# Hybrid encoder layer: expert rows added to the output by accumulating scatters, expert weights in 4 KB pieces, nested branches, hidden products transposed in the gate bank

## The chip, the cores and the metric

The kernel runs on one core of a Trainium2 chip, as one launch. The metric is the device time of that launch in microseconds (us). Engines are called as in the profile: PE (TensorE; PEld its weight loads), DVE (VectorE), ACT (ScalarE), POOL (GpSimd) and SP (SyncE, which here only issues DMAs). All data are float32.

## What is computed

One encoder layer over 512 tokens of width 1024: attention of two kinds, an output projection, and then a hierarchical mixture of experts. Each token picks one of 4 groups of experts, and two of the 4 experts in that group.

```python
def hier_moe(h, w_rg, b_rg, w_re, b_re, w_gate, w_up, w_down):
    ...
    pg_top, g_idx = lax.top_k(p_g, 1)                  # one group of 4
    ...
    pe_top, e_idx = lax.top_k(p_e, TOP_K_IN_GROUP)     # two experts in it
    wts = pg_top * pe_top / jnp.sum(pe_top, axis=-1, keepdims=True)
    ...
    a = jnp.einsum('bsd,edf->bsef', h, w_gate)
    u = jnp.einsum('bsd,edf->bsef', h, w_up)
    hid = jax.nn.silu(a) * u * combine[..., None].astype(h.dtype)
    return jnp.einsum('bsef,efd->bsd', hid, w_down)

x = x + mixed @ w_out[l]
h2 = rms_norm(x, g_ffn_norm[l])
x = x + hier_moe(h2, ...)      # 16 experts, D_EXPERT = 256, 512 tokens x 2 experts
```

## The kernel before

**Stages.** Up to about 340 us the kernel computes the projections, the two attentions and the output projection. Tokens stand in four blocks of 128 (T = 4); `x_sb[:, t, :]` holds the residual stream. Near the end of the attention, block by block, the router is computed: `logits_out(t)` picks group and experts, `ranks_out(t)` gives each token its slot in each of its two experts, and `dispatch(t)` (POOL, two indirect DMAs) scatters the normed rows `h2s[t]` to the DRAM tensor `slot_rows`.

**Items.** Every expert has CAP = 96 slots. The 16 x 96 slots are cut into ITEMS = 12 items of 128 slots; three items hold the 4 experts of one group. What doesn't fit goes to extra tiles of one expert each: 10 are provided for, the first (item 12, LAST) is always computed, the others stand under branches (`passes`). An item is four blocks of 32 slots, each with the weights of its own expert.

**An item on the engines.** PE: `x_turns` (8 transposes of the gathered rows, L1401), `gate_up` (64 matmuls, L1416), `hid_turns` (2 transposes of the hidden products, L1424), `down` (32 matmuls, L1437). ACT: silu (L732) and the left half of y out of the bank (`left_y`, L738). DVE: `x_read` (L1074), `hidden` (L1083), `hidden_read` (L1090), `right_y` (L1097). ACT issues the load of the item's rows (L722) and the store of y to the DRAM tensor `expert_rows` (L743). y_sb has two buffers. PE runs the items in this order:

```python
x_turns(0)
for g in range(LAST + 1):
    gate_up(g)
    if g < LAST:
        x_turns(g + 1)
    if g > 0:
        down(g - 1)
    hid_turns(g)
down(LAST)
```

**Weights.** SP loads an expert's gate and up weights (`load_gu`, L367, 2048 KB) and down weights (`load_dn`, L371, 1024 KB) into a ring of RING = 5 experts. A load is issued when the last item that uses the buffer's former expert has run its matmuls. A partition's 16 KB (8 KB for down) are one piece.

**The end.** When the last y is stored, POOL goes through the branches of the extra tiles (L313, L315) and gathers for each token block its two rows of `expert_rows` (8 indirect DMAs, L575); DVE multiplies each by its weight and adds it to `x_sb` (8 instructions, L1125); SP stores the four blocks to `out` (L438). The weights come from `weights_out(t)` (L954 to L957: four small DVE instructions), which before run inside item 1. Early on, two DMAs zero `slot_rows` and most of `expert_rows`. The order is written by hand; engines wait on semaphores.

## Time and profile before

| | us |
|---|---|
| median of 3 runs (571.57 to 580.37) | 573.88 |
| profiled execution | 577.23 |
| its span, first to last instruction | 575.5 |
| PE busy in the span | 498.2 |
| end of the last matmul | 541.87 |

The profiled execution has 1.73 us around its span. Stage times below are microseconds from the span's start.

### The profile page before, as it was taken

What the parts mean: (1) busy time and instruction counts of PE and PEld (TensorE: products, weight loads), DVE (VectorE), ACT (ScalarE), POOL (GpSimd) and SP (SyncE); (2) the same over time, 40 slices, a digit from 0 to 9 for tenths busy, and PEclk for the clock granted to TensorE, in tenths of its full rate; (3) what the DMA queues carried; (4) which work ended last, traced back from release to release, by engine and by line L of the source; (5) the groups of instructions that cost most, each with busy time, mean ns of one, the idle gap of its engine ahead of it and who ended that gap; (6) DMA issues with size and microseconds to landing.
All of it is one profiled execution on the core that took longest, in us unless ns stands there. A gap on an engine that the chain in (4) does not pass through costs nothing.

```text
span 575.5 us, 7543 instructions
## 1 busy us (share of the span) xinstructions
PE 498.2 (87%) x2858; PEld 262.2 (46%) x2858; DVE 232.8 (40%) x591; ACT 112.0 (19%) x273; POOL 134.7 (23%) x150
## 2 busy tenths in 40 slices
PE   5898899999989999999999969369999999999600
PEld 3553544445656676655666655323333333333100
DVE  1127345505697534544455653333421122211133
ACT  2200332233213343313223220300000001000100
POOL 2211388732899100000010211303100000000050
PEclk9999899999998999999999967559999999999955
DMA  8999910006000000470002493636999999970165
GB/s 303 422 386 420 422 56 0 1 1 235 1 1 1 0 1 2 183 329 1 0 1 71 160 354 105 241 110 202 338 419 423 424 425 423 427 303 38 76 235 209
DMA packets 21501, 111.53 MB, mean 194 GB/s; under 512 B 3152, under 2 KB 4688, under 8 KB 16720
## 3 DMA queue, kind: packets, MB, share of 16 engines
q1 hardware_dynamic: 13680, 88.68, 38.5%
q10 hardware_dynamic: 4320, 13.83, 6.1%
q0 software_dynamic: 3456, 8.39, 4.1%
q8 instruction: 31, 0.51, 0.4%
q14 instruction: 14, 0.11, 0.1%
HBM read 81.53 MB, written 33.55 MB: 200 GB/s over the span
## 4 chain that ended last, share of the span: by engine, by line
PE 74%; DVE 7%; issue 4%; DMA 3%; ACT 1%; POOL 1%; POOLq 1%; DVEq 0%; ACTq 0%
PE bank L1416 17%; PE bank L1164 12%; PE bank L1302 10%; PE bank L1437 8%; PE bank L1139 7%; PE bank L1226 5%; PE bank L1240 4%; PE bank L1267 3%; PE bank L1199 3%; PE bank L1401 2%; DMA arena<-expert_rows,small 2%; PE bank L1254 1%; POOL arena L575 1%; PE bank L1424 1%; PE bank L1316 1%
## 5 line engine op out<-in xcount | busy, mean ns | idle before, releaser
L1164 PE MATMUL bank<-arena 128*128 128x512 f32 (+1 forms) x256 | 115.2, 589 | 5.5 <-DVE arena L783 3.1
L1416 PE MATMUL bank<-arena 128*32 128x512 f32 x832 | 96.3, 608 | 1.4 <-DVE arena L1074 0.8
L1139 PE MATMUL bank<-arena 128*128 128x128 f32 (+1 forms) x412 | 61.0, 284 | 20.8 <-DVE arena L865 4.6
L1164 PEld LDWEIGHTS bank<-arena 128*128 128x128 f32 x256 | 49.6, 196 | 61.4 <-issue 54.6
L1139 PEld LDWEIGHTS bank<-arena 128*128 128x128 f32 (+1 forms) x412 | 50.2, 144 | 56.9 <-issue 42.8
L1302 PE MATMUL bank<-arena 128*128 128x512 f32 x128 | 63.5, 624 | 0.0
L1416 PEld LDWEIGHTS bank<-arena 128*32 128x32 f32 x832 | 27.0, 112 | 61.4 <-issue 59.9
L865 DVE COPY arena<-bank 128x512 f32<-128x512 f32 (+2 forms) x64 | 36.2, 586 | 35.7 <-PE bank L1139 35.7
L1437 PE MATMUL bank<-arena 128*32 128x512 f32 x416 | 47.4, 595 | 0.8 <-DVE arena L1090 0.8
L575 POOL DMA_INDIRECT arena<-expert_rows,small x8 | 8.4, 1053 | 144.8 <-issue 144.8
L457 POOL TENSOR_SCALAR small<-small 128x1 f32<-128x1 f32 x16 | 3.7, 232 | 157.5 <-ACT arena L638 95.8
L1083 DVE TENSOR_TENSOR arena<-arena,bank 128x256 f32<-128x256 f32 x13 | 5.5, 421 | 82.2 <-ACT arena L732 76.8
L1226 PE MATMUL bank<-arena 96*128 96x512 f32 x64 | 35.2, 634 | 1.0 <-ACT arena L624 1.0
L473 POOL TENSOR_TENSOR arena<-arena 128x512 f32<-128x512 f32 (+2 forms) x20 | 22.1, 1119 | 59.1 <-issue 18.9
L674 ACT ACTIVATE arena<-bank,small 128x512 f32<-128x512 f32 x32 | 22.0, 687 | 70.4 <-DVE small L969 70.3
L969 DVE TENSOR_REDUCE small<-bank 128x1 f32<-128x512 f32 x32 | 22.0, 686 | 33.7 <-PE bank L1226 33.7
L1302 PEld LDWEIGHTS bank<-arena 128*128 128x128 f32 x128 | 22.9, 197 | 22.1 <-issue 22.1
L1240 PE MATMUL bank<-arena 128*128 128x64 f32 x256 | 32.3, 270 | 0.0
L453 POOL TENSOR_TENSOR small<-small 128x24 f32<-128x24 f32 (+2 forms) x7 | 29.8, 4261 | 6.5 <-DVE small L823 3.5
L1240 PEld LDWEIGHTS bank<-arena 128*128 128x128 f32 x256 | 31.2, 192 | 0.2 <-issue 0.2
L783 DVE TENSOR_TENSOR arena<-bank,small 128x512 f32<-128x512 f32 (+1 forms) x28 | 18.1, 666 | 28.8 <-PE bank L1139 28.7
L732 ACT ACTIVATE arena<-bank 128x256 f32<-128x256 f32 x13 | 5.0, 383 | 124.1 <-PE bank L1416 124.1
(148 smaller groups left out, 506.3 us busy)
## 6 DMA issues: line engine op xcount, KB each, us to landing
arena<-in_w_gu SPq DMA_DIRECT2D x17, 2048.0 KB, 13.8
arena<-in_w_dn SPq DMA_DIRECT2D x17, 1024.0 KB, 13.8
slot_rows<-arena SPq DMA_DIRECT2D x1, 11264.0 KB, 36.3
arena<-slot_rows ACTq DMA_DIRECT2D x13, 512.0 KB, 9.5
expert_rows<-arena ACTq DMA_DIRECT2D x13, 512.0 KB, 10.1
expert_rows<-arena SPq DMA_DIRECT2D x1, 4608.0 KB, 45.5
arena<-in_w_out SPq DMA_DIRECT2D x2, 2048.0 KB, 8.2
arena<-in_x SPq DMA_DIRECT2D x4, 512.0 KB, 10.8
```

The source lines that it names most:

```text
L453: nc.gpsimd.tensor_tensor(v, v, mhalf[:, 0:n], ALU.pow).then_inc(s_root, 1)
L473: nc.gpsimd.tensor_tensor(dst, src, src, ALU.mult).then_inc(s_sqr, 1)
L674: nc.scalar.activation(Pb[u % 2], SB[u % 2][:, :], ACT.Exp, bias=nmax[:, u % 2, h:h + 1], accum_out=ssum[:, t % 2, 0, h:h + 1]).then_inc(s ...
L865: nc.vector.tensor_copy(PT[u % 2][:, 0:blocks, :], TPB[p % 2][:, 0:blocks * P].rearrange("p (a b) -> p a b", a=blocks))\
L969: nc.vector.tensor_reduce(nmax[:, u % 2, u % H:u % H + 1], SB[u % 2][:, :], AX.X, ALU.max, negate=True).then_inc(s_mx, 1)
L1139: last = nc.tensor.transpose(TPB[p % 2][0:s.shape[-1], b * P:(b + 1) * P], s, ident)
L1164: last = nc.tensor.matmul(product_bank(i)[:, 0:width], hT[:, k, t * P:(t + 1) * P], w[:, k, :], start=(k == 0), stop=(k == KD - 1))
L1226: nc.tensor.matmul(SB[u % 2][:, :], qT[:, h, t * P:(t + 1) * P], kT[:, h, :], start=True, stop=True).then_inc(s_S, 1)
L1240: last = nc.tensor.matmul(OB[t % 2][:, h * DV:(h + 1) * DV], PT[u % 2][:, k, :], v_sb[:, k, h * DV:(h + 1) * DV], start=(k == 0), stop=(k ...
L1302: last = nc.tensor.matmul(YB[b][:, :], src[:, k, :], w_o[half][:, k, b * 512:(b + 1) * 512], start=(k == 0), stop=(k == 3))
L1416: last = nc.tensor.matmul(GU[g % 2][BLK * b:BLK * (b + 1), :], xT[g % 2][:, k, BLK * b:BLK * (b + 1)], w_gu[n % RING][:, k, :], start=(k = ...
L1437: last = nc.tensor.matmul(YR[g % 2][half][BLK * b:BLK * (b + 1), :], hidT[g % 2][:, k, BLK * b:BLK * (b + 1)], w_dn[n % RING][:, k, half * ...
```

## The change

**Output by accumulating scatters.** SP stores `x_sb` to `out` right after the output projection. Each item's y is multiplied by its row's weight when it leaves PSUM (`left_y`, `right_y`, now with `tag_sb[:, g, 1:2]` as scale) and POOL then adds the rows to `out` by indirect DMAs with `compute_op=ALU.add` (`add`). Row number and weight reach the slot's partition as "tags": POOL scatters pairs (row, weight) to a DRAM tensor `slot_tags` just as it scatters the rows, and ACT reads them back (`load_tags`). An item mixes two experts, in which the same token can stand twice, so each item has two adds ("runs"), one for each expert; the rows of the other have their number pushed out of bounds by a constant (`K_CUT`) and are skipped. Adds of different experts in a group are kept apart by waits (`added`). y_sb has three buffers, released by the adds. `expert_rows`, the gathers L575, the DVE adds L1125 and the stores after them are gone, and so is the zeroing of `expert_rows`. `weights_out(t)` moves from item 1 to behind `ranks_out(t)`, with its exponentials (`top_exps`) on ACT.

**Weights in pieces of 4 KB.** The host lays them out so that each partition's 16 KB (8 KB) are four (two) pieces.

**Nested branches.** The branches of the extra tiles are nested; the first that isn't taken skips all.

**Gate bank.** `hid_turns` writes into the gate half of the item's own bank `GU[g % 2]`. `x_turns(1)` writes to `YR[1]` and comes ahead of `gate_up(0)`; from then on `x_turns` run two items ahead, behind `down`, and ACT loads an item's rows four ahead.

```diff
-        y_sb = [at(110, D_MODEL), at(114, D_MODEL)]
-        y_back = [[at(kb + 4 * i, D_MODEL) for i in (0, 1)] for kb in (16, 24, 48, 56)]
+        y_sb = [at(110, D_MODEL), at(114, D_MODEL), at(136, D_MODEL)]
...
+        def added_before(g):
+
+            return 16 * sum(2 if i < ITEMS else 1 for i in range(g % 3, g, 3))
...
-            for i in range(1, EXTRA):
-                with eng.If(tiles > i):
+            with ExitStack() as more:
+                for i in range(1, EXTRA):
+                    more.enter_context(eng.If(tiles > i))
                     extra(ITEMS + i)
...
-            sp.dma_start(y_dram[(ITEMS + 1) * P:, :].rearrange("(r p) d -> p r d", p=P),
-                         zero.unsqueeze(1).to_broadcast([P, EXTRA - 1, D_MODEL])).then_inc(s_zero, 16)
+            sp.wait_ge(s_fill, 1)
+            sp.dma_start(tag_dram.rearrange("(p r) c -> p (r c)", p=P), tag_fill).then_inc(s_zero, 16)
...
-                sp.dma_start(w_gu[n % RING].rearrange("p k f -> p (k f)"),
+                sp.dma_start(w_gu[n % RING].rearrange("p (q k) f -> p q (k f)", q=4),
...
             sp.wait_ge(s_y, len(groups))
             load_gu(4, 4)
+            for t in range(T):
+                sp.wait_ge(s_x1, group["b", t, 1] + 1)
+                sp.dma_start(out[t], x_sb[:, t, :]).then_inc(s_out, 16)
...
-            for t in range(T):
-                sp.wait_ge(s_fin, t + 1)
-                sp.dma_start(out[t], x_sb[:, t, :]).then_inc(s_out, 16)
             sp.wait_ge(s_out, 16 * T)
+            sp.wait_ge(s_add[LAST % 3], added_before(LAST) + 16)
...
+            def dispatch_tags(t, of, done, rows):
+                for k in range(TOP):
+                    nc.gpsimd.indirect_dma_start(
+                        out=tag_dram, out_offset=bass.IndirectOffsetOnAxis(ap=of[:, t, k:k + 1], axis=0),
+                        in_=tags[:, t, k, :], in_offset=None,
+                        bounds_check=rows * P - 1, oob_is_err=False).then_inc(done, 16)
+
+            def early_tags(t):
+                pool.wait_ge(s_wts, t + 1)
+                dispatch_tags(t, slots[0], s_tagged, ITEMS)
...
             dispatch(3)
+            for t in range(T):
+                early_tags(t)
...
+                dispatch_tags(t, slots[1], s_over, TILES)
+
+            pool.wait_ge(s_out, 16 * T)
+
+            def add(g, run):
+                pool.wait_ge(s_ya, g + 1)
+                pool.wait_ge(s_yv, g + 1)
+                pool.wait_ge(s_tok, 1 if g < ITEMS else 2)
+                nc.gpsimd.indirect_dma_start(
+                    out=out_rows, out_offset=bass.IndirectOffsetOnAxis(ap=tag_row[:, run, g:g + 1], axis=0),
+                    in_=y_sb[g % 3], in_offset=None,
+                    bounds_check=SEQ - 1, oob_is_err=False, compute_op=ALU.add).then_inc(s_add[g % 3], 16)
+
+            def added(g, run):
+
+                pool.wait_ge(s_add[g % 3], added_before(g) + 16 * (run + 1))
+
+            for g in range(0, ITEMS, 3):
+                add(g, 0)
+                added(g, 0)
+                add(g, 1)
+                add(g + 1, 0)
+                added(g, 1)
+                added(g + 1, 0)
+                add(g + 1, 1)
+                add(g + 2, 0)
+                added(g + 1, 1)
+                added(g + 2, 0)
+                add(g + 2, 1)
+            added(LAST - 1, 1)
+            add(LAST, 0)
...
-            for t in range(T):
-                for k in range(TOP):
-                    nc.gpsimd.indirect_dma_start(
-                        out=y_back[t][k], out_offset=None, in_=y_dram,
-                        in_offset=bass.IndirectOffsetOnAxis(ap=slots[2][:, t, k:k + 1], axis=0),
-                        bounds_check=(ITEMS + EXTRA) * P - 1, oob_is_err=False).then_inc(s_back[t], 16)
...
+            act.wait_ge(s_tagged, 16 * TOP * T)
+            load_tags(0, ITEMS)
...
+                act.wait_ge(s_tag, 16 if g < ITEMS else 32)
+                if g >= 3:
+                    act.wait_ge(s_add[g % 3], added_before(g))
+                nc.scalar.activation(y_sb[g % 3][:, 0:512], YR[g % 2][0][:, :], ACT.Copy,
+                                     scale=tag_sb[:, g, 1:2]).then_inc(s_ya, 1)
...
                 hidden(g)
-                if g < LAST:
-                    x_read(g + 1)
                 if g > 0:
                     right_y(g - 1)
+                if g + 2 <= LAST:
+                    x_read(g + 2)
                 hidden_read(g)
                 if g == 0:
                     slots_out()
-                if g == 1:
-                    for t in range(T):
-                        weights_out(t)
+                    tag_rows(0, ITEMS)
+                if g == LAST - 1:
+                    tag_rows(ITEMS, TILES)
...
             x_turns(0)
+            x_turns(1)
             for g in range(LAST + 1):
                 gate_up(g)
-                if g < LAST:
-                    x_turns(g + 1)
                 if g > 0:
                     down(g - 1)
+                if g + 2 <= LAST:
+                    x_turns(g + 2)
                 hid_turns(g)
             down(LAST)
```

**What moves on POOL.** Ahead, POOL's rows of before from the dispatch of the last two blocks to the end of its straight code (L538 is `dispatch`, L561 the second scatter of the rows that didn't fit, L313 and L315 the first branch).

```order
L538 DMA slot_rows<-arena,small 2816x1024 x4
L561 DMA slot_rows<-arena,small 2816x1024 x8
L313 TENSOR_LOAD small
L313 ISA x2
L315 COMPARE_AND_BRANCH
```

And the same place of the change (L551 is `dispatch`, L558 `dispatch_tags`, L587 the second scatter of rows, L599 `add`).

```order
L551 DMA slot_rows<-arena,small 2816x1024 x4
L558 DMA slot_tags<-small 2816x2 x8
L587 DMA slot_rows<-arena,small 2816x1024 x2
L558 DMA slot_tags<-small 2816x2 x2
...
L599 DMA out<-arena 512x1024 x25
L324 TENSOR_LOAD small
L324 ISA x2
L327 COMPARE_AND_BRANCH
```

POOL gets 8 tag scatters behind the dispatch, 8 more among the second scatters (the pair of rows stands four times in all), and 25 adds ahead of the branches.

**What moves on PE.** PE's rows of before from the start of the expert stage (the two last matmul groups of the router end above it).

```order
L1401 MATMUL bank<-arena 128x128 x8
L1416 MATMUL bank<-arena 32x512 x32
L1401 MATMUL bank<-arena 128x128 x8
L1424 MATMUL bank<-arena 128x128 x2
L1416 MATMUL bank<-arena 32x512 x32
L1401 MATMUL bank<-arena 128x128 x8
L1437 MATMUL bank<-arena 32x512 x16
L1424 MATMUL bank<-arena 128x128 x2
```

And of the change (L1463 is `x_turns`, L1478 `gate_up`, L1485 `hid_turns`, L1498 `down`).

```order
L1463 MATMUL bank<-arena 128x128 x16
L1478 MATMUL bank<-arena 32x512 x32
L1463 MATMUL bank<-arena 128x128 x8
L1485 MATMUL bank<-arena 128x128 x2
L1478 MATMUL bank<-arena 32x512 x32
L1498 MATMUL bank<-arena 32x512 x16
L1463 MATMUL bank<-arena 128x128 x8
L1485 MATMUL bank<-arena 128x128 x2
```

Item 1's transposes now stand ahead of the first gate matmuls, and each later item's one place earlier; the last items have none left to do (where the trace counts 64 gate matmuls and 32 down matmuls for an item, the order counts 32 and 16).

**What moves on DVE.** DVE's rows of before from the slots of block 1 to the attention output of block 3 (L948 ends `ranks_out(1)`, L874 and L877 are `attn_out(1, 3)`, L783 the reads of the transposes).

```order
L948 CAST small<-small 128x2
L874 RECIPROCAL small<-small 128x8
L877 TENSOR_TENSOR arena<-bank,small 128x512
L783 TENSOR_TENSOR arena<-bank,small 128x512
```

And of the change (L1006 ends `ranks_out(1)`, L1012 to L1015 are `weights_out(1)`, L932 and L935 `attn_out(1, 3)`).

```order
L1006 CAST small<-small 128x2
L1012 TENSOR_SCALAR arena<-arena 128x1
L1013 TENSOR_TENSOR arena<-arena 128x1
L1014 RECIPROCAL small<-arena 128x1
L1015 TENSOR_TENSOR small<-small,arena 128x1
L932 RECIPROCAL small<-small 128x8
L935 TENSOR_TENSOR arena<-bank,small 128x512
L841 TENSOR_TENSOR arena<-bank,small 128x512
```

Four small instructions come between the ranks of block 1 and the attention output of block 3.

## Rows read from the trace of the kernel before

**Rows 1.** The page's busy times and shares of the span.

```profile
PE 498.2 (87%) x2858; PEld 262.2 (46%) x2858; DVE 232.8 (40%) x591; ACT 112.0 (19%) x273; POOL 134.7 (23%) x150
```

**Rows 2.** Stages: start:end, length, busy by engine, granted clock, DMA share, GB/s.

```profile
360.00:380.00 20.00, 7.44 (x40) 6.92 (x40) 5.66 (x39) 4.61 (x15) 4.05 (x5) 0.56 0.64 246
420.00:440.00 20.00, 20.00 (x182) 6.81 (x178) 4.26 (x8) 1.35 (x3) 0.00 (x0) 1.00 1.01 420
480.00:500.00 20.00, 20.00 (x186) 6.81 (x182) 4.26 (x8) 1.35 (x3) 0.00 (x0) 1.00 1.02 427
540.00:576.00 36.00, 1.83 (x20) 0.32 (x12) 10.96 (x9) 0.58 (x1) 8.43 (x8) 0.59 0.53 193
```

**Rows 3.** Chain that ended last, expert stage: start us, us, what.

```profile
371.12 3.31 DMA slot_rows<-arena,small
...
377.98 1.95 PE bank L1401 x8
...
380.70 9.92 PE bank L1416 x64
...
418.91 7.00 PE bank L1416 x64
425.91 1.02 PE bank L1401 x8
426.94 3.57 PE bank L1437 x32
430.50 0.37 PE bank L1424 x2
...
502.67 7.00 PE bank L1416 x64
...
538.19 3.69 PE bank L1437 x32
541.90 0.70 DVE arena L1097
...
542.67 3.15 DMA expert_rows<-arena
...
558.37 9.45 DMA arena<-expert_rows,small
```

**Rows 4.** DMA issues at 328, 371, 548 and 474 us: op xcount, KB each, us to landing.

```profile
slot_rows<-arena,small POOLq DMA_INDIRECT x1, 10.7
...
slot_rows<-arena,small POOLq DMA_INDIRECT x1, 3.3
...
arena<-expert_rows,small POOLq DMA_INDIRECT x1, 4.4
...
arena<-in_w_gu SPq DMA_DIRECT2D x1, 2048.0 KB, 15.8
```

**Rows 5.** DMA issues by line, from the page.

```profile
arena<-in_w_dn SPq DMA_DIRECT2D x17, 1024.0 KB, 13.8
arena<-slot_rows ACTq DMA_DIRECT2D x13, 512.0 KB, 9.5
expert_rows<-arena ACTq DMA_DIRECT2D x13, 512.0 KB, 10.1
```

**Rows 6.** Tile expert_rows from 400 us on, stores and gathers together: times to landing.

```profile
DMA to landing us min/median/max: 2.6/7.6/11.9
```

**Rows 7.** Timeline of POOL from 396 us: start, us, instruction, idle before.

```profile
396.35 0.96 POOL L561 DMA_INDIRECT slot_rows<-arena,small  x1 [24.27 <-DVE small L1066]
...
405.23 0.96 POOL L561 DMA_INDIRECT slot_rows<-arena,small  x1 [0.30 <-issue]
```

**Rows 8.** Timeline of DVE at the moved instructions and at the end.

```profile
342.42 0.17 DVE L948 CAST small<-small 128x2 int32<-128x2 f32 x1
342.49 0.20 DVE L874 RECIPROCAL small<-small 128x8 f32<-128x8 f32 x1
...
408.82 0.14 DVE L954 TENSOR_SCALAR arena<-arena 128x1 f32<-128x1 f32 x1
...
537.11 0.69 DVE L1097 COPY arena<-bank 128x512 f32<-128x512 f32 x1 [2.60 <-PE bank L1437]
```

More of the change, by code:

```diff
@@ L166, in build @@
         logits = sm(T, E)
-        wts = sm(T, TOP)
-        slots = [sm(T, TOP).bitcast(i32) for _ in range(3)]
+        tags = sm(T, TOP, 2)
+        tag_fill = sm(2 * TILES)
+        slots = [sm(T, TOP).bitcast(i32) for _ in range(2)]
         slot_f = sm(3, T, TOP)
@@ L986, in _ @@
             dve.wait_ge(s_k, 16)
+            for k in range(TOP):
+                link(nc.vector.tensor_copy(tags[:, :, k, 0], konst[:, K_ROW:K_ROW + T]))
             dve.wait_ge(s_bm, 1)
@@ L1018, in _ @@
                     ranks_out(RANKS_AT[s])
+                    weights_out(RANKS_AT[s])
             attn_out(1, T - 1)
@@ L1026, in _ @@
             ranks_out(2)
+            weights_out(2)
             logits_out(T - 1)
             ranks_out(T - 1)
+            weights_out(T - 1)
             def extras_out():
@@ L1094, in right_y, with tag_rows @@
                 dve.wait_ge(s_dn, 2 * g + 2)
-                if g >= 2:
-                    dve.wait_ge(s_yst[g % 2], 16 * (g // 2))
-                nc.vector.tensor_copy(y_sb[g % 2][:, 512:1024], YR[g % 2][1][:, :]).then_inc(s_yv, 1)
+                if g >= 3:
+                    dve.wait_ge(s_add[g % 3], added_before(g))
+                nc.vector.tensor_scalar(y_sb[g % 3][:, 512:1024], YR[g % 2][1][:, :], tag_sb[:, g, 1:2], None,
+                                        ALU.mult).then_inc(s_yv, 1)
+            def tag_rows(lo, hi):
+                dve.wait_ge(s_tag, 16 if lo == 0 else 32)
+                if lo == 0:
+                    for run in range(2):
+                        cut = konst[:, K_CUT + run * ITEMS:K_CUT + (run + 1) * ITEMS]
+                        last = nc.vector.tensor_tensor(tag_row[:, run, lo:hi], tag_sb[:, lo:hi, 0], cut, ALU.add)
+                else:
+                    last = nc.vector.tensor_copy(tag_row[:, 0, lo:hi], tag_sb[:, lo:hi, 0])
+                last.then_inc(s_tok, 1)
             x_read(0)
+            x_read(1)
             extras_out()
@@ L1109, in _ @@
                     slots_out()
-                if g == 1:
-                    for t in range(T):
-                        weights_out(t)
+                    tag_rows(0, ITEMS)
+                if g == LAST - 1:
+                    tag_rows(ITEMS, TILES)
             right_y(LAST)
@@ L1121, in _ @@
             passes(dve, extra_dve)
-            for t in range(T):
-                dve.wait_ge(s_back[t], 32)
-                for k in range(TOP):
-                    ins = nc.vector.scalar_tensor_tensor(x_sb[:, t, :], y_back[t][k], wts[:, t, k:k + 1],
-                                                         x_sb[:, t, :], ALU.mult, ALU.add)
-                    if k == 0:
-                        link(ins)
-                ins.then_inc(s_fin, 1)
         @block.tensor
@@ L1388, in _ @@
                 pe.wait_ge(*bank_read(p))
[L1390 to L1393 removed]
             def x_turns(g):
+                into = YR[1] if g == 1 else TPB
                 pe.wait_ge(s_xg[g % 3], 16 * (g // 3 + 1))
                 for b in range(2):
[L1398 removed]
+                    if g >= 2:
+                        pe.wait_ge(s_te, turn_x(g - 1 if g > 2 else 0, b) + 1)
                     for i in range(4):
                         k = 4 * b + i
[L1401 removed]
+                        last = nc.tensor.transpose(into[b][:, i * P:(i + 1) * P], xg[g % 3][:, k * P:(k + 1) * P], ident)
                     last.then_inc(s_tt, 1)
```

97 lines of the change are left out of this document (50 added, 47 removed).

## Prediction

> **What bounds the kernel now.** I read the page's busy times first. PE is busy 87% of the span [rows 1], but a share over the whole span hides its last part. So next the busy times by stage: from 420 to 500 us PE is busy without a gap at full clock, and so are the DMAs (420 and 427 GB/s, share 1.01 and 1.02); from 540 on PE has 1.83 us of work in 36 us [rows 2]. The expert stage is thus two things: a body in which PE is the bound, with the DMAs just under theirs, and a tail without PE.
>
> The chain of waits gives the sizes. An item costs PE 7.00 (gate and up) + 1.02 (transposes of x) + 3.57 (down) + 0.37 (hidden transposes) = 11.96 us, and three items, one group of experts, 35.9 us [rows 3]. Nothing else stands in the chain there. The last matmul ends at 541.87, y leaves PSUM by 542.6, and its store lands 3.15 us later [rows 3]. Then POOL's branches, 8 gathers one after the other, the last of which takes 9.45 us to land at 567.8 [rows 3], DVE's adds, and the last store of the output, up to 575.5. From the last matmul to the end of the span that is 575.5 - 541.87 = 33.6 us. With 1.73 us around the span the profiled execution is 577.23; it lies 0.6% above the median of 573.88. I make the sum against 577.23 and move the difference to the median.
>
> **The change, part by part.**
>
> *The tail.* All of those 33.6 us go: branches, gathers, DVE adds and output stores. What comes in their place is the end of a chain of adds. PE's end matters less than the code's order on POOL: item 11's y is complete at 537.11 + 0.69 = 537.8 [rows 8], and from there stand add(11,0), a wait until it has landed, add(11,1), a wait, and add(12,0), whose landing ends the program. Item 12's y is there at 542.6, before its turn comes. So the tail is 3 D from 537.8, where D is the time from the issue of an add to its landing, its issue (some 1 us) included.
>
> *D with idle DMAs.* No row shows an accumulating DMA. The nearest is the plain scatter of 128 rows at 371 us, 3.3 us; a gather of 128 rows from DRAM took 4.4 us [rows 4]. An add must read the destination as well as write it. Below, it could be as fast as the scatter, 3.3 (an add here carries at most 96 valid rows, not 128; cheaper still is not excluded, but the write and its receipt stay). Above, reading and writing one after the other in full, 3.3 + 4.4 = 7.7. I take 4.5, near the plain scatter, as rows are fewer and read and write overlap from row to row. Tail: 3 x 4.5 = 13.5 us, bounds 9.9 and 23.1.
>
> *D beside the weight loads.* In the body the adds run beside saturated DMAs. The scatter at 328 us, beside weight loads in 16 KB pieces, took 10.7 us, and y's stores 10.1 [rows 4, 5]. With 4 KB pieces a row of 4 KB waits for less of a weight at each turn, so D should fall, while the accumulation adds. Bounds: 4.5 (idle) and 10.7 + 4.4 = 15.1; I take 8. What does the schedule tolerate? Per group POOL has three waits and three issues that aren't covered by them (1.27 us from one to the next [rows 7]): 3 D + 3.8 us, against PE's 35.9. They balance at D = 10.7. Adds start late: POOL must first issue the 16 scatters of rows and tags from 396.35 on, 16 x 1.27 = 20.3 us, so until 416.7 [rows 7], while item 0's y is ready at about 405. At D = 8 a group takes POOL 27.8 us, so the 12 us are made up within two groups. Three y buffers cover this: item 3's y, at about 442, needs item 0's adds, landed by 416.7 + 2 x 8 = 433. The body hides the adds; without that cover they cost what the rivals say.
>
> Here the Trainium skill, page "DMA: Bandwidth & Descriptors", section "Queues, rings and completion order", bears on the case: each DMA engine goes round its queues and switches only between packets. The 10.7 us beside loads against 3.3 alone agree with it. By that rule alone, with 8 rows of 4 KB on each of 16 engines and a 4 KB weight piece between each two, D would be an estimated 5 to 6 us, and the sum would stay as it is.
>
> *DMA load of the body.* Before, a group moves 4 x 3072 KB of weights, 3 x 512 KB in and 3 x 512 KB out: 15.7 MB in 35.9 us would be 438 GB/s; the DMAs gave 420 to 427 [rows 2, 5], so weights fall about 1 us further behind with each group. That is affordable: a gate load issued as gate_up(7) ends, at 473.8, lands 15.8 us later [rows 4], at 489.6, and is wanted by gate_up(10) at 502.7 [rows 3]. 13 us are the smallest of these margins. Now y's stores (1.57 MB per group) give way to adds of valid rows only: 1024 rows in four groups, at most 256 x 4 KB = 1.05 MB per group. Counted twice for the read of the destination that is 2.1 MB, 16.2 MB in all, 38.2 us at 425 GB/s: 1.2 us per group more than before, 4 us over the stage, inside the 13. Cost zero; pieces of 4 KB I count neither as faster nor slower, since rows of x and y are already that size at full rate.
>
> *PE's order.* x_turns(1) now stands ahead of gate_up(0), at half clock: gate_up(0) starts about 1.2 us later than 380.70, but PE no longer waits out the reads between 379.9 and 380.7, and 1.02 us of transposes behind gate_up(0) are replaced by those of item 2. I count the start at zero. Every later item has its transposes one place earlier, so one set of 1.02 us drops out between gate_up(1) and the end of item 11: -1.0 us on y(11). The hidden transposes in the gate bank change no duration.
>
> *Moved small work.* weights_out(1) comes between L948 and L874, which follow each other on the chain [rows 8]. Four instructions of about 0.15 us, linked, from 408.82 on at some 0.2 us each: +0.8 us. weights_out(2) falls into a DVE gap of 1.3 us before block 3's logits, weights_out(0) into a PE-bound stretch, weights_out(3) behind the last slots: 0. The stores of x_sb to out, 2 MB or 5 us of DMA time, queue behind load_gu(4) from about 358 and are through by about 371, when the last dispatch scatter starts; the DMAs are only 64% busy from 360 to 380 [rows 2]. Some of it may lie before that scatter: +0.3, bounds 0 and 1.5. If that cover is gone, it is on the path, as PE waits there for the scatter and the load of x [rows 3].
>
> *Tags.* 8 tag scatters run on POOL from 372.1 to 382.5 and land by about 386; ACT waits for them ahead of silu(0), which is wanted only when gate_up(0) ends at about 391. The read-back is 1536 pieces of 8 bytes, a size no row has. It has until about 404, when y(0) leaves PSUM: 18 us. Zero, bounds 0 and 5. Less zeroing of DRAM lies far from the path: zero.
>
> *Sum.* y(11) ready: 537.8 - 1.0 + 0.8 + 0.3 = 537.9. Adds: + 13.5 = 551.4. Plus 1.73: 553.1, which is 24.1 us less than 577.23. From the median: 573.88 - 24 = **550 us**.
>
> **Rivals.**
>
> *A. Adds fall behind (same side, smaller gain).* If D beside the loads is 12 to 17 us, a group takes POOL 40 to 55 us. At 14, the group starts are 416.7, 462.5 and 508.3; after that the loads are over and the rest runs at 4.5 us each, ending near 560, while y(6), ready at 478, waits until item 3's adds land at 490, and DVE's waiting y copy holds back the hidden copy behind it. Span 560 to 570, or a median of about 562. The 10.7 us of [rows 4] without any accumulation speaks for it, the smaller pieces against it. Its sister is DMA capacity: were an add worth five plain passes, a group would need 19.4 MB, 45.7 us, and three groups would fall behind by 29 us against 13 us of margin: 16 us of PE stall, about 566. The Trainium skill, same page, section "Where 436 GB/s comes from", puts the limit of DRAM traffic per core near 358 GB/s; by it 16.2 MB need 45 us, the same sister case. The 427 GB/s of [rows 2] contradict it, so I give it no more than its part in A.
>
> *B. Slower.* One mechanism: the serial chain of adds, in the body. It decides from D = 18 us on: a group takes POOL 57.8 us, groups start at 416.7, 474.5 and 532.3, the y buffers stall PE, so that the loads last until about 540, and the remaining eight steps at 4.5 us plus issues end near 588. That is 2% over 575.5. The same comes out if accumulation is slow in itself, beside loads or not: the chain ends at 430.5 + 14 D, which passes 587 at D = 11.2. Nothing in the trace is that slow for 0.5 MB; y's stores reach at most 11.9 [rows 6].
>
> *C. It doesn't do what it says.* If the adds were cheap, but the last were queued behind something, the tail would stay above 25 us. I see nothing queued there: all loads have landed by 515 or so. It shares in A.
>
> *D. Faster still.* D = 3.3 in the tail, and the 2.1 us that gate_up(2) loses in before recovered by shorter queues: 550 - 3.6 - 2.1 = 544.
>
> **How the numbers follow.** The forecast with D from 3.3 to 7.7 in the tail spans 546 to 560: chance 0.68. A with C 0.16 (560 to 575), B 0.10, D 0.03, anything else 0.03. The range 543 to 565 takes the forecast, D and the better half of A. 2% is about what a measurement of this kernel can tell from no change. Faster by more than that, under 562.4: 0.68 + 0.03 + a third of A and others, 0.77; within 2% 0.12; slower 0.11.
>
> **What the profile after would show.** The last matmul near 541; three DMA waits of POOL behind it in the chain, each 3 to 8 us; no L1125. PE without gaps from 420 on: gaps ahead of `down` or `hid_turns` with DVE waiting for an add mean A or B, gaps ahead of `gate_up` mean late weights. The adds' time to landing in the body tells 8 from 12 or more. A gap on ACT before silu(0) would mean late tags. The prediction is wrong if one accumulating scatter costs over 8 us with idle DMAs or over 11 us beside loads.

## The result, and the profile after

| | before | after |
|---|---|---|
| median of 4 runs each, same chip (us) | 577.03 | 564.29 |
| ratio, 95% interval | | 0.985 [0.982, 0.989] |
| profiled execution (us) | 577.23 | 565.41 |
| its span | 575.5 | 563.7 |
| end of the last matmul | 541.87 | 539.38 |
| from there to the end of the span | 33.6 | 24.3 |

The kernel became 1.5% faster, [1.1%, 1.8%]: 8.5 us of 577, where the prediction said 24. Two of the four runs before, 580.18 and 580.37, were in a slower state of the chip, so the ratio is to the other two (median 572.7). The direction is right, the size is a third; the 564.29 lies at the upper end of the stated range of 543 to 565. In the profiled pair 11.8 us of span went: 2.5 before the last matmul, 9.3 behind it. Stage by stage, the view answering to [rows 2] (the columns are the same):

```profile
PE 493.7 (88%) x2858; PEld 264.0 (47%) x2858; DVE 223.5 (40%) x587; ACT 113.8 (20%) x273; POOL 180.7 (32%) x184
...
360.00:380.00 20.00, 6.82 (x42) 6.33 (x42) 7.86 (x48) 4.36 (x8) 8.63 (x10) 0.62 0.83 302
420.00:440.00 20.00, 20.00 (x186) 6.56 (x182) 4.07 (x9) 1.46 (x3) 5.44 (x4) 1.00 1.03 370
480.00:500.00 20.00, 20.00 (x190) 6.49 (x182) 4.91 (x10) 1.67 (x4) 6.16 (x4) 1.00 1.04 384
540.00:564.00 24.00, 0.00 (x0) 0.00 (x0) 0.75 (x1) 0.69 (x1) 6.16 (x4) 0.54 0.20 27
```

In the body PE has no gap, as before. The DMAs are busy the whole time as before, but they move 370 and 384 GB/s where they moved 420 and 427. In the last 24 us there is no matmul; POOL issues four adds, and the DMAs are 20% busy. So the work that is left there is small, and something waits in line. The timeline of POOL says what. Its columns: start, duration, instruction, and in brackets the idle time before it and what ended it.

```profile
419.75 0.98 POOL L558 DMA_INDIRECT slot_tags<-small  x1 [0.30 <-issue]
421.03 1.59 POOL L599 DMA_INDIRECT out<-arena  x1 [0.30 <-issue]
433.08 1.57 POOL L599 DMA_INDIRECT out<-arena  x1 [10.46 <-DMA out<-arena]
...
458.31 1.54 POOL L599 DMA_INDIRECT out<-arena  x1 [0.30 <-issue]
469.84 1.54 POOL L599 DMA_INDIRECT out<-arena  x1 [9.98 <-DMA out<-arena]
471.68 1.54 POOL L599 DMA_INDIRECT out<-arena  x1 [0.30 <-issue]
482.69 1.54 POOL L599 DMA_INDIRECT out<-arena  x1 [9.47 <-issue]
484.54 1.54 POOL L599 DMA_INDIRECT out<-arena  x1 [0.30 <-issue]
495.01 1.54 POOL L599 DMA_INDIRECT out<-arena  x1 [8.93 <-issue]
496.85 1.54 POOL L599 DMA_INDIRECT out<-arena  x1 [0.30 <-issue]
...
543.32 1.54 POOL L599 DMA_INDIRECT out<-arena  x1 [3.69 <-DVE arena L1158]
545.16 1.54 POOL L599 DMA_INDIRECT out<-arena  x1 [0.30 <-issue]
549.32 1.54 POOL L599 DMA_INDIRECT out<-arena  x1 [2.62 <-DMA out<-arena]
554.86 1.54 POOL L599 DMA_INDIRECT out<-arena  x1 [4.00 <-DMA out<-arena]
```

The rows from 458.31 to 496.85 are one group, items 3 to 5, with the two adds of each item: 38.5 us, made of three waits (from one add's start to the next 11.5, 11.0 and 10.5) and three issues of 1.84 us that nothing covers. `add(g, r)` is the add of item g's run r. PE takes 3 x 11.68 = 35.0 us for the same items. The adds start at 421.03, 13 us after item 0's y is there (407.75), and instead of catching up they stay behind. The last four rows are add(10,1), (11,0), (11,1) and (12,0). Item 11's y has been complete since 535.35, the end of the first of these two rows of DVE:

```profile
534.60 0.75 DVE L1158 TENSOR_SCALAR arena<-bank,arena 128x512 f32<-128x512 f32 x1 [2.60 <-PE bank L1498]
...
542.31 0.75 DVE L1158 TENSOR_SCALAR arena<-bank,arena 128x512 f32<-128x512 f32 x1 [6.62 <-DMA out<-arena]
```

add(11,0) starts at 545.16. **The lag is 9.8 us**, and the program ends later by it; some 0.8 us of it are the time that POOL needs after a y even when it stands ready (below). The second row shows it too: item 12's y waits 6.62 us with the matmuls done, because its buffer is held by the adds of item 9. From 445 to 500 us an add takes this long to land:

```profile
DMA to landing us min/median/max: 9.1/9.5/10.8
```

The start of the expert stage also moved. PE's rows of after, against 377.98 and 380.70 in [rows 3]:

```profile
383.98 3.65 PE L1463 MATMUL bank<-arena 128*128 128x128 f32 x16 [11.80 <-DMA arena<-slot_rows]
387.55 7.53 PE L1478 MATMUL bank<-arena 128*32 128x512 f32 x64
```

It begins 6.0 us later, yet PE ends 2.5 us earlier: from the first of these transposes to the last matmul 155.4 us against 163.9.

### The profile page after: what moved, and what is told of

The parts are those of the page before. It is cut to its first block and busy times, and to the rows that moved or that the text cites. A ratio compares the mean times of both kernels' runs of the same rounds, so it can differ in the third digit from the quotient of the medians.

```text
span 563.7 us, 7565 instructions
## 1 busy us (share of the span) xinstructions
PE 493.7 (88%) x2858; PEld 264.0 (47%) x2858; DVE 223.5 (40%) x587; ACT 113.8 (20%) x273; POOL 180.7 (32%) x184
## 5 line engine op out<-in xcount | busy, mean ns | idle before, releaser
L1478 PE MATMUL bank<-arena 128*32 128x512 f32 x832 | 92.4, 596 | 0.0
L599 POOL DMA_INDIRECT out<-arena x25 | 38.6, 1543 | 97.1 <-issue 45.8
L1478 PEld LDWEIGHTS bank<-arena 128*32 128x32 f32 x832 | 25.7, 110 | 57.3 <-issue 57.0
L1498 PE MATMUL bank<-arena 128*32 128x512 f32 x416 | 47.0, 592 | 0.8 <-DVE arena L1151 0.8
L1290 PE MATMUL bank<-arena 96*128 96x512 f32 x64 | 36.5, 657 | 1.0 <-ACT arena L674 1.0
L1158 DVE TENSOR_SCALAR arena<-bank,arena 128x512 f32<-128x512 f32 x13 | 9.8, 751 | 53.9 <-DMA out<-arena 38.3
## 6 DMA issues: line engine op xcount, KB each, us to landing
arena<-in_w_dn SPq DMA_DIRECT2D x17, 1024.0 KB, 19.7
arena<-in_x SPq DMA_DIRECT2D x4, 512.0 KB, 10.7
```

What stands on the lines that cost most here:

```text
L599: nc.gpsimd.indirect_dma_start(out=out_rows, out_offset=bass.IndirectOffsetOnAxis(ap=tag_row[:, run, g:g + 1], axis=0), in_=y_sb[g % 3], i ...
L1290: nc.tensor.matmul(SB[u % 2][:, :], qT[:, h, t * P:(t + 1) * P], kT[:, h, :], start=True, stop=True).then_inc(s_S, 1)
L1478: last = nc.tensor.matmul(GU[g % 2][BLK * b:BLK * (b + 1), :], xT[g % 2][:, k, BLK * b:BLK * (b + 1)], w_gu[n % RING][:, k, :], start=(k = ...
L1498: last = nc.tensor.matmul(YR[g % 2][half][BLK * b:BLK * (b + 1), :], hidT[g % 2][:, k, BLK * b:BLK * (b + 1)], w_dn[n % RING][:, k, half * ...
```

## The experiments

All ran against the kernel before; a ratio without other words is to it. The spans, landings and stage times are each from one traced execution. In the diffs, `-` and `+` are against the changed kernel unless said otherwise. In kernels with lines moved, `add` is L599, L600, L602, L605 or L607.

### Weights in one piece again

```diff
-                sp.dma_start(w_gu[n % RING].rearrange("p (q k) f -> p q (k f)", q=4),
+                sp.dma_start(w_gu[n % RING].rearrange("p k f -> p (k f)"),
...
-                sp.dma_start(w_dn[n % RING], row(w_dn_d, e)).then_inc(s_wdn[n % RING], 16)
+                sp.dma_start(w_dn[n % RING].rearrange("p k d -> p (k d)"), row(w_dn_d, e)).then_inc(s_wdn[n % RING], 16)
```

> The changed kernel with the expert weights in pieces of 16 KB and 8 KB again, all else kept. Two theories on why the adds take 9 to 10 us beside the weight loads, where 8 were forecast. Queue theory (a row of an add waits for one piece of a weight at each turn): with 16 KB pieces the adds beside the loads rise to 13 to 17 us, a group of three items takes POOL 47 us or more, y's copies wait longer and the span grows by 10 to 25 us over 563.7. Load theory (the DMAs are simply full and the size of a piece doesn't matter): adds stay at 9 to 10 us, time within 1%.

580.6 us, ratio 1.014 [1.006, 1.022]; span 579.1. Its POOL timeline, and the landing of the adds from 430 to 500 us:

```profile
456.75 1.54 POOL L599 DMA_INDIRECT out<-arena  x1 [11.92 <-issue]
458.60 1.53 POOL L599 DMA_INDIRECT out<-arena  x1 [0.30 <-issue]
472.46 1.53 POOL L599 DMA_INDIRECT out<-arena  x1 [12.33 <-issue]
...
570.28 1.54 POOL L599 DMA_INDIRECT out<-arena  x1 [3.77 <-DMA out<-arena]
```
```profile
DMA to landing us min/median/max: 8.0/12.5/13.6
```

The first wait is 21.6 us (12.1 in the changed kernel), those up to 516 us are 10.8 to 14.4, 13.1 in the mean, instead of 11.0; items 3 to 5 take 43.8 us (474.30 to 518.14), and the y buffers stall PE (16.88 us busy of the 20 from 480 on; last matmul 560.5): DVE's copy of y waits up to 15 us for an add, and PE for DVE's next copy. An add waits behind pieces of weights, and its landing follows their size. The pieces are what keeps this change on the good side: rivals A and B of the prediction describe this kernel.

### Plain scatters

```diff
-                    bounds_check=SEQ - 1, oob_is_err=False, compute_op=ALU.add).then_inc(s_add[g % 3], 16)
+                    bounds_check=SEQ - 1, oob_is_err=False).then_inc(s_add[g % 3], 16)
```

The output then lacks the sum over a token's experts and the residual.

> The changed kernel with plain scatters in place of the accumulating ones: rows overwrite the output, so the sum over a token's experts and the residual are left out. Accumulation theory (the read of the destination doubles the DMA work of a row): adds beside the loads fall from 9.5 to 6 or 7 us, a group takes POOL under 30 us, the adds keep up with PE, the tail's three fall from 3.3, 4.8 and 6.2 to about 3.3 each, and the span comes to about 549 to 552. Rival (queueing alone sets it): adds stay near 9 us and the span within 3 us of 563.7.

551.9 us, ratio 0.960 [0.954, 0.966]; span 550.5. The instruction takes 0.96 us instead of 1.54, and from 430 to 500 us the scatters land like this:

```profile
DMA to landing us min/median/max: 7.0/8.9/9.6
```

So most of the 9.5 us is there without accumulation, beside the weights. But the little that is saved, 0.6 us on each of six instructions and some tenths on each wait of a group, puts items 3 to 5 at 34.0 us (453.40 to 487.40), under PE's 35.0; the scatters catch up by 522 us, and the lag is gone. The span is 13.2 us less than after's: 5.7 of it is a shorter tail (12.8 us from the scatter of (11,0) to the end, against 18.5), the rest is the lag, less a start that was 2 us later (386.04). So the changed kernel stands close to its balance.

### Adds started early

The scatters of rows and tags that didn't fit, 16 instructions ahead of the first add, are taken apart: block 0's stay ahead, the others go into the waits of the first adds.

```diff
                 add(g, 0)
+                if g == 0:
+                    overflow(1)
                 added(g, 0)
                 add(g, 1)
                 add(g + 1, 0)
+                if g == 0:
+                    overflow(2)
                 added(g, 1)
                 added(g + 1, 0)
                 add(g + 1, 1)
                 add(g + 2, 0)
+                if g == 0:
+                    overflow(3)
```

> The changed kernel with the second scatters of rows and tags spread over the waits of the first adds: 4 ahead of the first add, 4 behind each of the next three issues. Lag theory (the adds start 13 us late, at 421 for a y that is ready at 407.7, and never make it up, since a group takes POOL 38.5 us against PE's 35.0): the first add goes out near 408, the lag at item 11 falls from 9.8 us to 0 to 2, and the span to 553 to 556. Rival (full DMAs set the pace of the adds, an earlier start only meets more contention): adds get slower, lag at item 11 stays above 7 us, span above 561.

556.2 us, ratio 0.967 [0.962, 0.973]; span 554.7, which is 9.0 us less than after. POOL at the end:

```profile
535.04 1.54 POOL L602 DMA_INDIRECT out<-arena  x1 [3.84 <-DVE arena L1167]
540.38 1.54 POOL L602 DMA_INDIRECT out<-arena  x1 [3.79 <-issue]
545.91 1.54 POOL L602 DMA_INDIRECT out<-arena  x1 [3.99 <-DMA out<-arena]
```

The first add starts at 406.60, 14.4 us earlier (2.8 of them because the stage itself began earlier here, at 381.19). add(11,0) at 535.04 is now released by DVE, 0.8 us after the end of its y's copy at 534.21, not by an add: the lag is gone but for the release, and the time with it. The 9.0 us add up: y(11) ready 1.1 earlier, the lag 9.8 to 0.8, the tail 1.1 longer (19.7 against 18.5). Neither the number of adds nor the tail's steps changed, so it was the lag that cost them.

### Output stores after the expert rows

```diff
             load_gu(4, 4)
+            sp.wait_ge(s_xg[2], 16)
             for t in range(T):
                 sp.wait_ge(s_x1, group["b", t, 1] + 1)
```

> The changed kernel with the stores of the residual to the output held back until the rows of item 2 have landed, so that they no longer run beside the last dispatch scatter (5.7 us from its issue to the load behind it, against 3.3 in the kernel before). Theory: the scatter returns to 3.3 to 3.6 us, PE's first transposes of the expert stage come 2 to 2.5 us earlier, and since the adds' chain starts from there too, the span falls by 2 to 2.5 us. Rival (the tag scatters behind it on the same queue slow it down): the scatter stays above 5 us and nothing moves.

562.6 us, ratio 0.980 [0.974, 0.987]; span 562.3. In time it is not to be told apart from the changed kernel. From the last dispatch scatter (373.83) to the first transposes (382.39) 8.56 us; in after 373.73 to 383.98, 10.25; in before 371.12 to 377.98, 6.86. From 365 to 375 us, where that scatter is issued, this kernel and then after:

```profile
365.00:375.00 10.00, 3.56 (x16) 3.49 (x16) 4.61 (x32) 2.06 (x5) 3.48 (x4) 0.50 0.53 212
```
```profile
365.00:375.00 10.00, 3.57 (x16) 3.49 (x16) 4.51 (x32) 2.06 (x5) 3.37 (x5) 0.50 1.01 377
```

The stores of `x_sb` keep the DMAs full (share 1.01) just when the scatter and the load of x are in line. In this pair they cost 1.7 us, not the 0.3 of the prediction: 2.3 us are won between the scatter and the load behind it (3.4 us instead of 5.7), and 0.6 lost again on the load. Single executions differ here: over all traces this stretch is 9.7 to 11.7 us with the stores early (four kernels) and 8.6 to 10.1 with them late (six), so their price is some 1 to 2 us. At least 1.7 us over before's 6.86 remain in each; they lie beside the tag scatters, which no run takes away.

### The three repairs together

Early adds, late output stores, and the tag scatters of blocks 0 and 1 ahead of `dispatch(3)`.

> The changed kernel with the second scatters spread over the first adds' waits, the stores of the residual to the output held back until item 2's rows are in, and two blocks' tags scattered ahead of the last dispatch. Theory (the lag of the adds and the slower dispatch scatter are separate losses, and both sit on the path): 0.967 of the kernel before for the early adds alone, less another 1.5 to 3 us: 0.962 to 0.965. Rival (held back, the stores of 2 MB meet the first adds or the tags delay them): 0.967 to 0.972.

556.48 us against 579.48, ratio 0.960 [0.954, 0.966]; span 553.6. PE and POOL:

```profile
381.00 3.28 PE L1475 MATMUL bank<-arena 128*128 128x128 f32 x16 [10.74 <-DMA arena<-slot_rows]
```
```profile
534.25 1.54 POOL L605 DMA_INDIRECT out<-arena  x1 [4.06 <-DVE arena L1170]
539.54 1.54 POOL L605 DMA_INDIRECT out<-arena  x1 [3.75 <-issue]
544.83 1.54 POOL L605 DMA_INDIRECT out<-arena  x1 [3.75 <-DMA out<-arena]
```

This is the fastest kernel that computes everything, 4.0% faster than before; from early adds alone it is not to be told apart in time. The early tags show no gain: from the last dispatch scatter (371.90) to these transposes 9.10 us, with late stores alone 8.56. PE waits once for weights, 1.67 us ahead of a `down`. The tail is three steps of 5.29, 5.29 and 8.8 us. In the last, the DMAs move data until 551, 6 us after the issue; 3 us more pass to the end of the span. In this kernel the waits from add(g,0) to add(g,1) are 9.3 to 10.8 us, 9.9 in the mean: 3 x (9.9 + 1.85) = 35.3 us a group, about PE's 35.0.

### Pieces of 2 KB

The same with `reshape(E, P, -1, D_MODEL // 2)` on the host and the loads cut to match.

> The same kernel as the run beside it (early adds, late stores of the residual, early tags), with the expert weights in pieces of 2 KB instead of 4 KB. Adds took a median of 12.5 us beside loads in pieces of 16 and 8 KB and 9.4 us beside pieces of 4 KB. Queue theory (an add's row waits for the piece ahead of it): 8 us or less beside the loads; with the lag already gone this moves the span by 0 to 2 us. Rival (smaller pieces cost the DMAs more per byte, and the weights come late): DMAs move under 350 GB/s in the body, PE waits for weights, span 3 us or more above the run beside it.

565.2 us, ratio 0.978 [0.970, 0.985]; span 563.4, last matmul 546.9. The queues from 430 to 500 us (packets, MB, share of the engines' time), for this kernel and then for the one with 4 KB:

```profile
q1 hardware_dynamic: 9737, 19.52, 74.1%
q0 software_dynamic: 2080, 2.53, 18.3%
```
```profile
q1 hardware_dynamic: 5409, 21.24, 75.6%
q0 software_dynamic: 2080, 2.53, 18.3%
```

The share of a queue x 16 engines x 70 us over its MB is the engines' time for a megabyte: 42.5 us of weights in 2 KB pieces, 39.9 in 4 KB, and 37.6 in 16 KB (in the kernel before with the new PE order, below: 23.39 MB at 78.6%). The same working for the kernel before gives 37.7, and 39.6 with 4 KB pieces as its only edit; only the first experiment (16 KB beside adds, with loads that pause) is out of order, 40.7. Smaller pieces cost the loads, and here PE waits for them, 1.8, 1.8 and 3.2 us; the adds gain little (waits of 7.7 to 10.1 us, 9.0 in the mean, against 9.9; the trace has no landings for this kernel).

### Pieces of 8 KB

> e7_best, with the weights in pieces of 8 KB (gate_up halves of 8 KB, down rows whole) instead of 4 KB. Theory of the queue (an add's rows wait behind pieces of weights, so their landing grows with the piece: 9.5 us beside 4 KB, 12.5 beside 16 and 8 KB): adds of about 11 us in the body, a group of six adds takes 38 to 42 us against 35 of matmuls, the adds fall behind, and the span is 3 to 10 us longer than e7_best's 553.6. Rival (fewer descriptors per byte: the DMA engines spend 37.6 us per MB at 16 KB against 39.6 at 4 KB, so the weights come sooner): span equal to e7_best's or up to 2 us shorter.

568.3 us, ratio 0.981 [0.974, 0.987]; span 567.0. The landing of the adds from 440 to 500 us, and PE at the place where it stops:

```profile
DMA to landing us min/median/max: 10.5/11.3/11.8
```
```profile
519.37 1.97 PE L1475 MATMUL bank<-arena 128*128 128x128 f32 x8 [8.82 <-DMA arena<-slot_rows]
```

The landing is the 11 us expected; the waits, 12 to 15 us, are longer than that, and what fills the difference isn't shown. Items 3 to 5 take 45.4 us (449.09 to 494.47). The damage is larger than forecast, 13.4 us of span against 3 to 10, through a path that I hadn't listed. The transposes at 519.37 are item 12's. ACT issued the load of their rows in time, right behind the read-back of the second set of tags, 1280 pieces of 8 bytes:

```profile
484.32 6.79 ACTq L788 DMA_DIRECT2D arena<-slot_rows  x1
```
```profile
arena<-slot_tags ACTq DMA_DIRECT2D x1, 10.0 KB, 32.1
```

The tags take 32.1 us to land and the rows behind them 35.0, until 519.3; so PE waits 8.8 us. The same read-back lands in 19.6 us beside pieces of 4 KB and in 12.7 beside 2 KB. (ACT's copies of y wait 7.3 and 9.8 us for a buffer, but only at 503 and 517, when this load is long issued.) With 16, 8, 4 and 2 KB the spans are 579.1 (without the repairs), 567.0, 553.6 and 563.4: of the sizes tried 4 KB is best.

### Accumulation by itself

The three repairs with plain scatters; the sums are missing from the output.

> e7_best, with the scatters plain instead of accumulating. It leaves the sum over the two experts of a token out of the output. It measures accumulation by itself when no add is behind any more. Theory (accumulation costs 0.57 us of instruction and about 1 to 2 us of landing in each of the three serial steps of the tail, nothing in the body): steps of 3.5 to 4 us in place of 5.3, span 548 to 550, and the last matmul stays at 537.4 within 0.5 us. Rival (DMA-engine time doubled by accumulation also slows the weights, so the matmuls end sooner too): last matmul 1 us or more earlier, span under 547. If accumulation costs nothing: 553 to 554.

548.9 us, ratio 0.951 [0.943, 0.958]; span 546.2.

```profile
533.36 0.97 POOL L605 DMA_INDIRECT out<-arena  x1 [6.50 <-DVE arena L1170]
536.29 0.97 POOL L605 DMA_INDIRECT out<-arena  x1 [1.97 <-issue]
539.71 0.97 POOL L605 DMA_INDIRECT out<-arena  x1 [2.45 <-DMA out<-arena]
```

From add(11,0) to the end of the span 12.8 us, against 19.35: 6.5 us for three serial steps. In the body the waits are 7.2 to 9.2 us (8.0 in the mean, against 9.9), and the last matmul ends at 536.5, 0.9 us sooner, though `gate_up(1)` began 1.0 us later: the wait of 1.67 us for weights is gone. Both theories had a part; accumulation costs 7.4 us of span here, of which 6.5 in the tail.

### One serial step less

Item 12's add goes to a tensor of its own, without waiting for add(11,1); its rows are missing from the output.

> e7_best, with one difference: the add of item 12's tile (12,0) goes to a DRAM tensor of its own and does not wait for the add before it. It leaves the overflow rows of item 12 out of the output. In e7_best the three last steps were 534.25, 539.54, 544.83 and the end at 553.6. Theory of the serial tail (the adds into one tensor stand in line, each one landing long): one step of 5.3 us goes, span 547 to 549. Rival (the end is set by the last landing and the matmuls' end at 537.4, so that (12,0) issued early changes little, or the last add of (11,1) takes the 8.8 us to the end whatever stands before it): less than 2 us of change, span 552 to 554.

```profile
540.48 1.54 POOL L607 DMA_INDIRECT out<-arena  x1 [1.31 <-DVE arena L1177]
546.24 1.54 POOL L607 DMA_INDIRECT out<-arena  x1 [4.22 <-issue]
548.09 1.54 POOL L637 DMA_INDIRECT side_rows<-arena  x1 [0.30 <-issue]
```

558.8 us (553.7 to 561.3), ratio 0.963 [0.955, 0.971]; the profiled span is 557.3. As a whole it says little: in this execution the first transposes stand at 388.80, 7.8 us later than in the kernel with the repairs; the granted clock was 0.96 from 120 to 160 us and 0.91 from 160 to 200, far from the edit, where the other has 1.00. Counted from add(11,0) to the end it is 16.8 us against 19.35: 2.5 of the 5.3 us go. The step before them took 5.76 us instead of 5.29, and the two adds under way together take longer than one alone (data move until 554, 7.8 us behind the first of them, against 6 us for one). Neither theory's number came out; in this one execution the serial wait was worth half of what it looks like.

### The kernel before with 4 KB pieces, and with the new PE order

First the one, then the other, each as the only edit to the kernel before. The second has `x_turns(1)` ahead of `gate_up(0)`, `x_turns(g + 2)` behind `down`, the hidden transposes in the gate bank and rows loaded four ahead.

> The kernel before with the expert weights in pieces of 4 KB, nothing else changed. Stores of y took 10.1 us beside pieces of 16 KB; queue theory: 7 us or less here, weight loads 3 to 6 us longer, PE without waits, time within 0.5% of before, since neither is on the path. Rival (pieces of 4 KB cost DMA time per byte): in the body the DMAs move under 410 GB/s where before moved 424, PE waits for late weights, time 0.5 to 2% above before.

577.2 us, ratio 0.998 [0.993, 1.003]. The page's DMA issues by line, answering to [rows 5]:

```profile
expert_rows<-arena ACTq DMA_DIRECT2D x13, 512.0 KB, 7.1
```

The stores of y land in 7.1 us instead of 10.1 and nobody gains by it, because nobody waits for them there.

> The kernel before with the change's order on PE (transposes two items ahead and behind the down matmuls, item 1's first of all), its banks (hidden transposes in the gate bank) and its load distance; output by gathers as before. From the first transposes to the last matmul before took 163.9 us and the change 155.4. Order theory: this part alone gives those 8.5 us: 156 us here, time 7 to 8.5 us (1.3%) below before. Rival (the body was faster because of shorter DMA queues, above all the 2.1 us that gate_up(2) lost): 160 us or more, gain under 4 us.

575.4 us, ratio 0.991 [0.987, 0.995]. Its first transposes and last matmul:

```profile
380.79 3.65 PE L1400 MATMUL bank<-arena 128*128 128x128 f32 x16 [8.23 <-DMA arena<-slot_rows]
...
535.09 3.64 PE L1435 MATMUL bank<-arena 128*32 128x512 f32 x32 [0.78 <-DVE arena L1092]
```

From the one to the end of the other 157.9 us, against 163.9 before and 155.4 after. So the order of PE is worth 6.0 of the 8.5 us that this stretch lost. They lie in three places. Up to the start of `gate_up(1)` 2.0 us are won, 12.7 us against 14.8: the granted clock stands at 0.50 until 386 us in both kernels, but with two sets of transposes first only some 1.5 us of `gate_up(0)` fall into that, where before 5.5 did, so it takes 7.80 us instead of the 9.92 of [rows 3]. Then an item takes 11.68 us from one `gate_up` to the next, where before it took 11.96, with the same instructions; over 11 items that is 3.1 us, and why it is shorter isn't shown. The rest, 0.8 us, is about the one set of transposes that drops out. The remaining 2.5 us are largely small gaps around `gate_up(2)`, about 2 us in the kernel before and in both of these, none in after; what closes them wasn't tried and stays open.

## Why the prediction was off

**What bounds the kernel now** stood. No row contradicts the reading of body and tail, and the 33.6 us behind the last matmul were the right stock to count.

**"D beside the weight loads ... I take 8"** was mis-sized, though inside its bounds: the landing is 9.5 us at the median. The argument had the right parts. Small pieces shorten a row's way through the queue (12.5 to 9.5 us for the adds, 10.1 to 7.1 for plain stores of y), and accumulation adds to it (8.0 to 9.9 us a wait). I took the first in full and too little of the second.

The sentence of the Trainium skill, page "DMA: Bandwidth & Descriptors", section "Queues, rings and completion order", that an engine changes queues only between packets, agrees with the order 12.5, 11.3, 9.5 of the landings beside pieces of 16, 8 and 4 KB. The 5 to 6 us that I estimated from it don't: 8.9 us were measured even for plain scatters. A quarter of the piece size took away a quarter of the landing, not three quarters; what the rest is made of no run here shows.

**"They balance at D = 10.7"** is the step that failed, together with 8. It took 1.27 us for an issue, from plain scatters [rows 7]; an accumulating one takes 1.54 + 0.30 = 1.84. And it let the next add start as the last one landed, while from a median landing of 9.5 us come waits of 10.5 to 11.5, since a wait ends with the slower of its adds (9.7 to 10.8 us) and POOL starts 0.8 us after that. With D as the wait, a group is 3 D + 5.5: 38.5 us at 11.0, and PE is down to 35.0. They balance at 9.8. I had 27.8 against 35.9, a cover of 8 us per group; in fact POOL was the slower one by 3.5 us. The sign that I gave for a wrong prediction, over 8 us for an add with idle DMAs or over 11 beside loads, hangs on the same balance: 5.3 and 9.5 us pass both, and the adds fell behind all the same.

**"The 12 us are made up within two groups"** followed from that and was wrong with it. The adds started at 421.0 (forecast 416.7; the stage began 6 us late), fell back from 13 us behind at item 0 to 19 at item 6 (496.85; its matmuls ended near 477), and only when the loads were through did they make up some, down to the 9.8 us that went into the tail. So **"The body hides the adds"** was false by little, 3.5 us per group, and early adds alone brought back 9.0 us of span.

**"Tail: 3 x 4.5 = 13.5 us, bounds 9.9 and 23.1"** measured 18.5 (545.16 to 563.7), inside the bounds: 4.2 and 5.5 us for two steps (5.3 and 5.3 without the lag), 8.8 for the last, as its landing takes 6.2 and behind it some 2.6 us pass that I didn't count. The sum in numbers: y(11) ready at 535.35 instead of 537.9, -2.55; lag +9.8; tail +5.05. Together +12.3, the span of 563.7 against 551.4.

**"PE's order ... I count the start at zero ... -1.0"** was too small: the order alone gave 6.0 us. The start, counted at zero, gave 2.0 of them; the 9.92 us of `gate_up(0)` in [rows 3], partly at half clock, I had before me. The shorter item gave 3.1, which nothing in the profile announced, and the set of transposes that drops out 0.8 for the 1.0.

Against that the stage began 6.0 us later (383.98 against 377.98). **"weights_out(1): +0.8"**: 0.65 (from the start of DVE's slot instructions to that of the attention output behind them 1.90 us instead of 1.25). 3.4 us lie between the last dispatch scatter and the first transposes. **"Out stores +0.3, bounds 0 and 1.5"** has 1.7 of them by the one pair of traces, just outside. **"Tags: zero"** holds for ACT's silu(0), but the load of item 0's rows took about 1 us longer beside them (379.44 to 383.98, 4.5 us against 3.5), which I hadn't priced; nor had I priced the second read-back, which costs nothing here and 8.8 us of PE with pieces of 8 KB. The last 2 us are no part of the change: the last dispatch scatter stands at 371.1 to 372.1 in the traces whose granted clock from 120 to 160 us is 1.00, and at 373.7 or later in those where it is 0.96, changed kernels among both.

**"DMA load of the body: cost zero"** held. The engines spend about 86 us per MB on adds against 44 on plain scatters (12.5% for 1.63 MB; for the plain ones the same working), which is the "counted twice" of the forecast. Loads of weights land in 24.5 us instead of 15.6, within the margin of 13 us; no matmul waits for weights. That pieces of 4 KB are "neither faster nor slower" is off by 5% (39.6 against 37.7 us per MB in the kernel before), off the path here.

**The rivals.** A is what happened, in a mild form: adds behind, and DVE's copy of y waiting up to 6.6 us, but no stall of PE. Its span, 560 to 570, contains the 563.7. I had written its condition as D from 12 to 17, with the balance at 10.7 assumed; with the balance at 9.8 it began at 10. B is the kernel with pieces of 16 KB, slower than before by 1.4%, with a wait of 13.1 us instead of the 18 that I asked for. In B I also wrote that nothing in the trace is as slow as 11.2 us for 0.5 MB; the 11.9 us of [rows 6] beside it are slower.

## What to carry to other kernels

Where a serial chain of DMAs is to be hidden behind compute, work out its period and the compute's period from the same kind of rows, with issue, landing and release of each step, and trust no thin cover: here 8 us in 36 on paper were 3.5 us too few in the trace. Beyond the balance a lag grows as long as the load lasts, and what is left of it comes out at the end. A late start of such a chain costs nothing if it has slack and everything if it hasn't; so start it as early as its data allow, and move other work of the issuing engine into its waits. The size of the pieces of a background load moves the latency of the small transfers beside it, and had a best value among those tried here, because small pieces cost the loads more time per byte.

## What the runs showed of the hardware

- An accumulating indirect scatter of 128 rows occupies POOL for 1.54 us, a plain one for 0.97, and the DMA engines for twice the time per byte (86 against 44 us per MB). With no loads beside it, it takes 4.2 to 5.8 us, mostly 5.3, from issue to the next issue that waits for it, the plain one 2.9 to 3.4.
- Median landing of an add beside full loads: 12.5 us with pieces of 16 KB, 11.3 with 8 KB, 9.5 with 4 KB; with 2 KB only the waits are known, 9.0 us against 9.9. The engines' time for a MB of weights: 37.6, 39.9 and 42.5 us at 16 (no adds beside), 4 and 2 KB.
- A read-back of 1280 pieces of 8 bytes (10 KB) beside full loads lands in 32.1, 19.6 and 12.7 us with pieces of 8, 4 and 2 KB. The issue of the next load on its queue takes ACT 6.79, 2.92 and 1.88 us then, where others take 0.39.
- Two independent adds at once end 7.8 us after the first is issued, one alone 6: a wait removed between them was worth half of a step. What they share no run shows.
